# Decoder step on one core: split-array products gathered into fewer interruptions of the dense matmul stream

## Chip, core, metric

One core of one Trainium2 chip runs the whole step. The metric is the device time of one execution, in microseconds (us). The chip's TensorE is called PE below, with its weight loads PEld; DVE is VectorE, ACT ScalarE, POOL GpSimd, SP the engine that issues DMAs.

## What is computed

One decoder layer on 512 prompt tokens and 8 sample tokens with 2048 tokens of past each:

```python
(conv), (q, k, v), (qd, kd, vd), gates = in_projection(rmsnorm(h), w_in)
y_a = conv_mixer(...)                      # gated width-3 convolution
z = q.k / 8 + b_h                          # stick-breaking attention, 8 heads, strictly causal
a = exp(log_sigmoid(z) + sum of log_sigmoid(-z) over later keys);  y_b = (a @ v) @ w_br_sb
y_c = combine of three dilated softmax windows (128,1), (512,4), (2048,16), 4 heads each
h = h + (g0*y_a + g1*y_b + g2*y_c) @ w_out
h = h + relu(rmsnorm(h) @ w_up)**2 @ w_down
```

The prompt attends to itself; the sample tokens attend to a paged pool of keys and values (16 pages of 128 tokens for each of 8 sequences) and to the window caches. Outputs are the new hidden rows and all new keys, values and window caches.

## The kernel before

**The dense stream.** Every weight matrix is cut into tiles of 128 output columns (a unit). fp32 products are made of three fp32r products (high x high, high x low, low x high), so a unit of 8 k-tiles for one half of the 520 tokens is 24 matmuls of 128x128 by 260 columns: one *tick*. A unit is two ticks. `TICKS` is the list of all ticks, in this order: sq, sk, sv (12 units), dq, dk, dv (18), convolution (12), gates, branches, out, MLP. Ticks 0 to 59 are the projections up to dv, ticks 60 to 83 the convolution's, 84 on the gates. ACT makes the high part of a weight tile, POOL or DVE the low part, DVE takes every tick's result from one of three PSUM banks G0 to G2.

**The interruptions.** Everything else that PE does is slipped between the two halves of a tick, or behind a tick. `make_plan` (from line 282) gives every such stage a due time in ticks; the list `PLAN` has one cell per half tick, and every engine walks through it. On PE the stages of one cell are sorted by `tensor_order` (`ARRAY_PARTS`, line 379): first transposes, then sums (`p_sum`, `l_sum`), then scores (`p_scores`, `l_scores`), then the products with pages and caches. A cell with work for PE is called an interruption below. There are 91.

Four shapes of product occur in them:
- *full*: transposes (`p_turn`, `l_turn`, `sv_rows`, `dv_rows`) and the bf16 mask product of identity and mask, 128x128;
- *64 columns* (128*64 in the profile): `p_sum(r)` adds up attention weights times values for two heads, `l_sum(m)` the same for a dilated step;
- *64 rows* (64*128): `p_scores(n)`, q.k for two heads, and `l_scores(m)`, one dilated step of two heads;
- *32 columns* (128*32): `dk(i)` (queries of the sample against two K tiles, 8 products of 512 columns), `v_sum(n)` (weights against one V tile, 4 products), `s_k`, `s_self`, `s_v`, `s_vself` (the windows of the sample).

A plain fp32 product is two records in the profile.

**Order of the prompt attention.** The sequence `PSEQ` has 32 heads times query blocks and four steps "d" for the sample's K pages. Step m has scores at tick 20 + m (for two heads at once, every second step), ACT's `p_weights` at +1, DVE's `p_scan` at +1, ACT's `p_exp` at +2, PE's `p_turn` at +3, and `p_sum` at +4 of the odd head. PSUM banks: scores in S0 and S1, transposes in TR, sums in OU, 32-column products in Z. The copies of the transposed weights, `pT`, are a ring of 3.

**The dilated part** has 16 steps from tick 61 on: `l_scores(m)` at 61 + m, logits (DVE), exponentials (ACT), `l_turn` at +2, `l_sum` at +3.

**Pages.** K and V pages and window caches go through four SBUF tiles `kv` of 1 MB. SP loads tile i when stage i - 4 has been used (`kv_load`, waiting for the semaphore `kv_used`); a tile of four pages is four DMAs, with the page numbers read from SBUF before. `DK_TICK` gives the ticks of the 16 `dk` stages by hand; the 32 `v_sum` come every 1.15 ticks from tick 53 to 90, each in a cell of its own.

```python
s_t = max(t + 1.0, at("dk", 5) + 1.5)
add(t + 4, "p_sum", n // 2)
t = int(v0 + 1.15 * i + 1.5 * (i // PAGES))
add(l0 + m, "l_scores", m)
add(l0 + m + 3, "l_sum", m)
```

Of the kernel before, what the change touches and what calls it, by code (L numbers as in the profile page):

```python
# [16 lines left out]
P = 128  # L17
# [99 lines left out]
def at(kind, tile, half=1):  # L117
    return AT[kind, tile, half]
# [153 lines left out]
for _n_ in range(QB * SBH):  # L272
    if _n_ in (0, 6, 16, 24):
        PSEQ.append(("d", len([1 for s in PSEQ if s[0] == "d"])))
    PSEQ.append(("p", _n_))
M_OF = {step: m for m, step in enumerate(PSEQ)}


DK_TICK = (10, 13, 15, 18, 21, 23, 25, 26, 30, 32, 34, 36, 39, 42, 44, 46)

# [4 lines left out]
def make_plan():  # L285

    plan = [[] for _ in range(2 * NT)]

    def add(tick, stage, n=0):
        plan[int(2 * tick) + 1].append((stage, n))  # L290

    t_kv = {}
    add(at("sq", 3) + 0.5, "qz")
    for i, t in enumerate(DK_TICK):
        add(t, "dk", i)
        t_kv[2 * i] = t_kv[2 * i + 1] = t
    add(at("dq", 5) + 1, "qd_zero")
    add(at("dk", 5) + 0.5, "qd")
    s_t = max(t + 1.0, at("dk", 5) + 1.5)
    for g in range(NG):  # L300
        add(s_t + g, "s_k", g)
        t_kv[KV_SK + g] = s_t + g
    add(s_t + 2.5, "s_self")
    add(s_t + 3, "s_log")
    add(s_t + 4, "s_soft")

    for i in range(QB):
        add(at("sv", 3) + 1.5 + i, "sv_rows", i)
    s0 = 20
    for m, (what, n) in enumerate(PSEQ):  # L310
        t = s0 + m
        if what == "p" and n % 2 == 0:
            add(t, "p_scores", n)
        add(t + 0.5, "p_weights", m)
        add(t + 1, "p_scan", m)
        add(t + 2, "p_exp", m)
        add(t + 3, "p_turn", m)
        if what == "p" and n % 2:
            add(t + 4, "p_sum", n // 2)
    p_end = s0 + len(PSEQ) + 4  # L320

    for g in range(NG):
        for r in range(2):
            add(at("dv", 5) + 1.5 + 2 * g + r, "dv_rows", 2 * g + r)
    add(at("dv", 5) + 1, "dvs")

    v0 = s_t + 4.5
    for i in range(2 * PAGES):
        t = int(v0 + 1.15 * i + 1.5 * (i // PAGES))
        add(t, "v_sum", i)  # L330
        t_kv[KV_V + i] = t
        if i % PAGES == PAGES - 1:
            add(t + 0.5, "v_out", i // PAGES)
            add(t + 2, "v_red", i // PAGES)
    v_end = t
    add(at("dv", 5) + 7.5, "s_turn")
    add(at("dv", 5) + 8.5, "s_vd")
    for g in range(NG):
        t = v_end + 1.5 + g
        add(t, "s_v", g)  # L340
        t_kv[KV_SV + g] = t
    add(t + 0.5, "s_vself")
    add(t + 1, "s_vout")
    add(t + 2.5, "s_red")

    l0 = max(p_end + 1, at("dv", 5) + 2)
# [70 lines left out]
def decoder_step(nc, x, o):  # L417

    ctx = ExitStack()
    with ctx:  # L420
# [56 lines left out]
        pw = place("pw", [P, 2, 512], R + 11408)  # L477
        pT = [place("pT0", [P, 512], R + 12432), place("pT1", [P, 512], c0 + 736), place("pT2", [P, 512], R + 21248)]

# [4 lines left out]
        bias = place("bias", [P, GH, BW], R)  # L484
        lT = place("lT", [P, 2, 512], R + 2048)
        o_sub = place("o_sub", [P, GH // 2, S], R + 3072)
# [77 lines left out]
        bias_in = sem("bias_in")  # L564
        l_made, l_pmade = sem("l_made"), sem("l_pmade")
        l_less, l_power, l_share_made, l_done = sem("l_less"), sem("l_power"), sem("l_share_made"), sem("l_done")
# [289 lines left out]
        def _(act):  # L856
# [171 lines left out]
            def l_turn(m):  # L1028
                cols = 2 * P * l_step(m)[3]
                copy(lT[:, m % 2, 0:cols], await_bank(act, "l_turn", m)[:, 0:cols]).then_inc(read["TR"], 1)  # L1030

# [144 lines left out]
        def _(dve):  # L1176
# [311 lines left out]
            def p_turn(m):  # L1488
                what, n = PSEQ[m]
                if what == "p":  # L1490
                    cols = P * (n // SBH + 1)
                    nc.vector.tensor_copy(pT[n % 3][:, 0:cols], await_bank(dve, "p_turn", m)[:, 0:cols]).then_inc(read["TR"], 1)

            def l_scores(m):
                jp, sub, i, blocks = l_step(m)
                n, end = P * blocks, BW if sub else 256
                if m == 0:
# [5 lines left out]
                for e in range(2):  # L1503
                    src = await_bank(dve, "l_scores", m, e)
                    stt(logits[:, e, :], src[:, 0:n], SCALE, bias[:, 2 * jp + e, end - n:end],
                        ALU.mult, ALU.add).then_inc(of(read, "l_scores", m, e), 1)
                for e in range(2):
                    await_taken(dve, "l_scores", m, e)
                nc.vector.tensor_reduce(lstat[:, 0, sub, i, 2 * jp:2 * jp + 2], logits, AX.X, ALU.max,
# [90 lines left out]
            def h_low(t):  # L1600
# [3 lines left out]

            stages = dict(p_scan=p_scan, p_turn=p_turn, l_scores=l_scores, l_stat=l_stat, l_mul=l_mul, v_out=v_out, s_log=s_log,
                          s_soft=s_soft, s_vout=s_vout, branch_split=branch_split)
# [33 lines left out]
        def _(pe):  # L1640
# [109 lines left out]
            def dk(i):  # L1750
# [14 lines left out]
                ins.then_inc(kv_used, 2)  # L1765

            def p_scores(n):
# [8 lines left out]
                for e in range(2):  # L1776
# [11 lines left out]
            def p_sum(r):  # L1788
# [5 lines left out]
                for b in range(i + 1):  # L1794
                    for e in range(2):
                        c = P * t + HD * e
                        ins = mm(dst[HD * e:HD * e + HD, P * t:P * t + P], sv_tok[:, b, c:c + HD],
                                 pT[(2 * r + e) % 3][:, P * b:P * b + P], b == 0, b == i, tile_position=(0, HD * e))
                if t == SBH // 2 - 1:
# [95 lines left out]

            def l_scores(m):
                jp, sub, i, blocks = l_step(m)
                if m == 0:
                    pe.wait_ge(dve_took, at("dk", 5) + 1)
                dst = [open_bank(pe, "l_scores", m, e) for e in range(2)]  # L1900
                queries = slice(P * i, P * i + P)
                keys = queries if sub else slice(P * (i + 1 - blocks), P * i + P)
                for n in range(2 if sub else 1):
                    for e in range(2):
                        t, rows = head(GH * (sub + n) + 2 * jp + e)
                        out = dst[e][:, P * n:P * n + P] if sub else dst[e][:, 0:P * blocks]
                        ins = mm(out, dqT[rows, t, queries], dkT[rows, t, keys], True, True)
                        if n == sub:
                            ins.then_inc(of(written, "l_scores", m, e), 1)

# [10 lines left out]
            def l_sum(m):  # L1921
# [7 lines left out]
                for b in range(blocks):  # L1929
                    g, rows = (1 + b, i) if sub else (0, i + 1 - blocks + b)  # L1930
                    for e in range(2):
                        d0 = 256 * g + HD * (2 * jp + e)
                        c = P * (blocks * e + b)
                        ins = mm(bank["OU"][HD * e:HD * e + HD, P * i:P * i + P], dv_tok[:, rows, d0:d0 + HD],
                                 lT[:, m % 2, c:c + P], b == 0, b == blocks - 1, tile_position=(0, HD * e))
                if m % QB == QB - 1:
# [22 lines left out]

            stages = dict(sv_rows=sv_rows, dv_rows=dv_rows, dk=dk, p_scores=p_scores, p_turn=p_turn, p_sum=p_sum,  # L1960
                          v_sum=v_sum, v_red=v_red, s_k=s_k, s_self=s_self, s_turn=s_turn, s_vd=s_vd, s_v=s_v,
# [175 lines left out]
```

## Time and profile before

| | |
|---|---|
| median of 3 runs | 1022.78 us (1021.09 to 1024.04) |
| profiled execution, first to last instruction (span) | 1019.7 us |
| time of that one execution as the runs count it | not listed apart; median less span is 3.1 us |
| PE busy | 998.8 us, 98% of the span |
| DVE, ACT, POOL busy | 586.0, 440.0, 312.0 us |
| mean granted clock of PE | 0.997 of full |
| DMA | 209.49 MB, 205 GB/s on average |

A busy PE record is longer than the step from one record to the next, since matmuls overlap; what a matmul costs the stream is the difference between its start and the next one's start. The timeline view prints those starts.

### The profile page before, as it was taken

How to read it: one execution, taken by the hardware profiler on the slowest of the kernel's cores; microseconds unless marked ns; L12 is line 12 of the kernel's file. 1: busy time of each engine (PE TensorE's matmuls, PEld its weight loads, DVE VectorE, ACT ScalarE, POOL GpSimd, SP SyncE). 2: the span in 40 equal slices, each digit the busy share in tenths (PEclk: the TensorE clock that was granted, in tenths of full speed). 3: DMA queues.
4: the chain of work that ended last, by engine and by line, in shares of the span. 5: the costliest groups of instructions: out<-in, count | busy, mean ns of one | idle time of the engine just before them, and what ended most of it. 6: DMA issues, size and time to landing. Idle time of an engine off the chain costs nothing.

```text
span 1019.7 us, 21807 instructions
## 1 busy us (share of the span) xinstructions
PE 998.8 (98%) x8426; PEld 912.7 (90%) x8426; DVE 586.0 (57%) x1042; ACT 440.0 (43%) x858; POOL 312.0 (31%) x180
## 2 busy tenths in 40 slices
PE   7999999999999999999999999999999999999996
PEld 6988787787877776899999999999999999999996
DVE  6215467879355457234445485577937956873334
ACT  6115556677244432234233323465436436434532
POOL 2333233222211221111112111144634355364720
PEclk9999999999999999999999999999999999999998
DMA  8589876785976467723322325456577487469102
GB/s 298 187 269 319 326 257 224 264 272 179 308 276 199 160 225 250 279 68 125 141 93 84 103 84 179 184 196 248 217 279 269 174 291 270 152 253 369 63 1 84
DMA packets 65672, 209.49 MB, mean 205 GB/s; under 512 B 7833, under 2 KB 10138, under 8 KB 63266
## 3 DMA queue, kind: packets, MB, share of 16 engines
q1 hardware_dynamic: 65282, 207.75, 57.9%
q8 instruction: 68, 1.11, 0.4%
q10 hardware_dynamic: 288, 0.35, 0.2%
q14 instruction: 34, 0.28, 0.1%
HBM read 200.59 MB, written 51.48 MB: 247 GB/s over the span
## 4 chain that ended last, share of the span: by engine, by line
PE 92%; DVE 3%; issue 1%; DMA 1%; SPq 1%; ACT 1%; DVEq 0%; ACTq 0%
PE G L1642 61%; PE S L1642 14%; PE Z L1642 13%; PE OU L1642 2%; PE TR L1645 2%; DMA kv<-in_kpool_dram 1%; DMA xraw<-in_xt_dram 1%; DVE mtmp L1188 1%; PE TR L1642 0%; DVE macc L1185 0%; DVE convy L1188 0%; SPq L720 0%; DVE pw L1483 0%; ACT mixh L865 0%; DVE wlo L1185 0%
## 5 line engine op out<-in xcount | busy, mean ns | idle before, releaser
L1642 PE MATMUL G<-xh,whi 128*128 128x260 f32 x1288 | 373.9, 290 | 8.1 <-DVE xl L1188 7.3
L1642 PE MATMUL G<-xl,whi 128*128 128x260 f32 x1288 | 364.9, 283 | 0.0
L1642 PE MATMUL G<-xh,wlo 128*128 128x260 f32 x1288 | 364.4, 283 | 0.0
L831 POOL TENSOR_TENSOR wlo<-wraw,whi 128x1024 fp32r<-128x1024 f32 x60 | 147.4, 2457 | 490.8 <-ACT whi L865 490.8
L1642 PEld LDWEIGHTS G<-xh,whi 128*128 128x128 f32 x1288 | 243.3, 189 | 52.2 <-issue 50.5
L1642 PEld LDWEIGHTS G<-xl,whi 128*128 128x128 f32 x1288 | 243.5, 189 | 0.0
L1642 PEld LDWEIGHTS G<-xh,wlo 128*128 128x128 f32 x1288 | 243.5, 189 | 0.0
L865 ACT ACTIVATE whi<-wraw 128x1024 fp32r<-128x1024 f32 (+1 forms) x84 | 88.0, 1048 | 226.1 <-PE G L1642 213.2
L827 POOL TENSOR_TENSOR wlo<-mraw,whi 128x512 fp32r<-128x512 f32 x60 | 81.6, 1382 | 95.1 <-ACT whi L865 95.1
L841 POOL TENSOR_TENSOR mlow<-mraw,bhigh 128x512 fp32r<-128x512 f32 x36 | 57.6, 1620 | 66.1 <-DVE bsum L1185 59.1
L1185 DVE TENSOR_TENSOR tg<-G,rstd 128x260 f32<-128x260 f32 x48 | 20.5, 428 | 85.8 <-PE G L1642 85.8
L1185 DVE TENSOR_TENSOR slow<-bsum,bhigh 128x512 fp32r<-128x512 f32 x48 | 60.1, 1252 | 3.0 <-ACT bhigh L865 3.0
L1642 PE MATMUL S<-xl,whi 128*128 128x260 f32 x176 | 49.7, 282 | 0.0
L1642 PE MATMUL S<-xh,whi 128*128 128x260 f32 x176 | 49.7, 282 | 0.0
L1642 PE MATMUL S<-xh,wlo 128*128 128x260 f32 x176 | 49.7, 282 | 0.0
L865 ACT ACTIVATE whi<-mraw 128x512 fp32r<-128x512 f32 (+1 forms) x62 | 36.3, 637 | 26.5 <-PE G L1642 9.5
L1483 DVE TENSOR_TENSOR_SCAN pw<-psp 128x512 f32<-128x512 f32 (+3 forms) x33 | 46.4, 1405 | 1.1
L1642 PE MATMUL G<-binh,whi 128*128 128x260 f32 x160 | 45.7, 285 | 1.3 <-issue 1.3
L923 ACT ACTIVATE tg<-tg,cvec 128x260 f32<-128x260 f32 x48 | 24.2, 505 | 49.5 <-DVE tg L1185 49.5
L1642 PE MATMUL G<-binh,wlo 128*128 128x260 f32 x160 | 45.3, 283 | 0.0
L1642 PE MATMUL G<-binl,whi 128*128 128x260 f32 x160 | 45.3, 283 | 0.0
L865 ACT ACTIVATE bhigh<-bsum 128x512 fp32r<-128x512 f32 x48 | 30.2, 630 | 32.4 <-DVE bsum L1185 32.0
(329 smaller groups left out, 2233.4 us busy)
## 6 DMA issues: line engine op xcount, KB each, us to landing
wraw<-in_w_in_dram SPq DMA_DIRECT2D x65, 512.0 KB, 5.8
kv<-in_kpool_dram SPq DMA_DIRECT2D x128, 256.0 KB, 3.8
kv<-in_vpool_dram SPq DMA_DIRECT2D x128, 256.0 KB, 3.5
mraw<-in_w_up_dram SPq DMA_DIRECT2D x32, 512.0 KB, 5.0
out_win_k_kept_dram<-in_cache_win_k_dram SPq DMA_DIRECT2D x8, 2047.0 KB, 11.4
out_win_v_kept_dram<-in_cache_win_v_dram SPq DMA_DIRECT2D x8, 2047.0 KB, 10.6
mraw<-in_w_down_dram SPq DMA_DIRECT2D x30, 512.0 KB, 3.4
wraw<-in_w_ab_dram SPq DMA_DIRECT2D x8, 512.0 KB, 3.3
```

The lines of the kernel that those rows point to most:

```text
L827: nc.gpsimd.tensor_tensor(low(u)[:, part], raw(u)[0][:, part], high(u)[:, part].bitcast(F32), ALU.subtract).then_inc(w_lo, 1)
L831: nc.gpsimd.tensor_tensor(low(u), raw(u)[0], high(u).bitcast(F32), ALU.subtract).then_inc(w_lo, 1)
L841: nc.gpsimd.tensor_tensor(block_low(g, j), block_raw(g, j), block_high(g, j).bitcast(F32), ALU.subtract).then_inc(b_lo_pool, 1)
L865: return nc.scalar.activation(out, in_, ACT.Copy, **kw)
L923: nc.scalar.activation(part, part, ACT.Tanh, scale=0.5, bias=bgate[:, g, t:t + 1]).then_inc(tanh_made, 1)
L1185: return nc.vector.tensor_tensor(out, a, b, op)
L1188: return nc.vector.scalar_tensor_tensor(out, a, scalar, b, op0, op1)
L1483: link(nc.vector.tensor_tensor_scan(w_[:, ::-1], l[:, ::-1], l[:, ::-1], carry, ALU.add, ALU.bypass))
L1642: return nc.tensor.matmul(out, lhsT, rhs, start=start, stop=stop, **kw)
L1645: return nc.tensor.transpose(out, in_, ident[0:rows, 0:rows])
```

## The change

Ticks of the plan: PSEQ's "d" steps move (8 in place of 6), `dk` 4 to 15 are put on ticks of `p_scores`; `p_sum` waits for the next cell that has split-array work (`TILED_TICKS`); the three `s_k` and `s_self` share tick 50, the three `s_v` and `s_vself` tick 92; V pages go in pairs, on three ticks of the prompt and on each pair of dilated steps, then every third tick; dilated steps go in pairs, with both steps' scores in one bank (columns 0 to 255 and 256 to 511) and both sums two ticks later. The mask product comes before the scores, which then add to it. `pT` is a ring of 5, `lT` of 3.

```diff
-    if _n_ in (0, 6, 16, 24):
+    if _n_ in (0, 8, 16, 24):
...
-DK_TICK = (10, 13, 15, 18, 21, 23, 25, 26, 30, 32, 34, 36, 39, 42, 44, 46)
+S0_TICK = 20
+SCORE_TICK = [S0_TICK + M_OF["p", 2 * r] for r in range(QB * SBH // 2)]
+TILED_TICKS = SCORE_TICK + [SCORE_TICK[-1] + 3, SCORE_TICK[-1] + 5]
+SUM_TICK = [min(t for t in TILED_TICKS if t >= SCORE_TICK[r] + 5) for r in range(QB * SBH // 2)]
+DK_TICK = [10, 13, 15, 18] + SCORE_TICK[0:12]
+PT_RING = 5
...
-    s_t = max(t + 1.0, at("dk", 5) + 1.5)
+    s_t = SCORE_TICK[13]
     for g in range(NG):
-        add(s_t + g, "s_k", g)
-        t_kv[KV_SK + g] = s_t + g
-    add(s_t + 2.5, "s_self")
+        add(s_t, "s_k", g)
+        t_kv[KV_SK + g] = s_t
+    add(s_t, "s_self")
...
         if what == "p" and n % 2 == 0:
+            add(t, "p_mask", n)
             add(t, "p_scores", n)
...
-            add(t + 4, "p_sum", n // 2)
+            add(SUM_TICK[n // 2], "p_sum", n // 2)
...
-    v0 = s_t + 4.5
+    l0 = max(p_end + 1, at("dv", 5) + 2)
+    v_ticks = [SCORE_TICK[-1]] + TILED_TICKS[-2:] + [l0 + 2 * q for q in range(LSTEPS // 2)]
+    while len(v_ticks) < PAGES:
+        v_ticks.append(v_ticks[-1] + 3)
     for i in range(2 * PAGES):
-        t = int(v0 + 1.15 * i + 1.5 * (i // PAGES))
+        t = v_ticks[i // 2]
         add(t, "v_sum", i)
...
     for g in range(NG):
-        t = v_end + 1.5 + g
+        t = v_end + 2
         add(t, "s_v", g)
...
-    for m in range(LSTEPS):
-        add(l0 + m, "l_scores", m)
-        add(l0 + m + 1, "l_weights", m)
-        add(l0 + m + 3, "l_sum", m)
-        if m % QB == QB - 1:
-            add(l0 + m + 3, "l_out", m // QB)
-        add(l0 + m + 2, "l_turn", m)
+    for q in range(LSTEPS // 2):
+        t = l0 + 2 * q
+        add(t, "l_scores", q)
+        for m in (2 * q, 2 * q + 1):
+            late = 0.5 * (m % 2)
+            add(t + late, "l_logits", m)
+            add(t + 1 + late, "l_weights", m)
+            add(t + 2 + 2 * late, "l_turn", m)
+            add(t + 4, "l_sum", m)
+            if m % QB == QB - 1:
+                add(t + 4, "l_out", m // QB)
...
+            def p_mask(n):
+                keys = P * (n // SBH + 1)
+                for e in range(2):
+                    dst = open_bank(pe, "p_scores", n + e)
+                    mm(dst[:, keys - P:keys], identb[:], maskb[:], True, True)
...
-                dst = [open_bank(pe, "p_scores", n + e) for e in range(2)]
                 for e in range(2):
                     t, rows = head((n + e) % SBH)
-                    mm(dst[e][:, 0:keys], sqT[rows, t, P * i:P * i + P], skT[rows, t, 0:keys], True, False)
-                for e in range(2):
-                    mm(dst[e][:, keys - P:keys], identb[:], maskb[:], False,
-                       True).then_inc(of(written, "p_scores", n + e), 1)
+                    dst = bank[SPOT["p_scores", n + e][0]]
+                    mm(dst[:, 0:keys], sqT[rows, t, P * i:P * i + P], skT[rows, t, 0:keys], False, True,
+                       skip_group_check=True).then_inc(of(written, "p_scores", n + e), 1)
...
-                        if n == sub:
-                            ins.then_inc(of(written, "l_scores", m, e), 1)
+                            if m % 2 and n == sub:
+                                ins.then_inc(of(written, "l_scores", q, e), 1)
```

DVE's stage that makes the logits, before called `l_scores` too, is now `l_logits`; it reads columns 256 * (m % 2) on, and frees the bank after the second step.

## Rows read from the trace of the kernel before

**Rows 1.** The page: busy time by engine, and the granted clock in 40 slices.

```profile
PE 998.8 (98%) x8426; PEld 912.7 (90%) x8426; DVE 586.0 (57%) x1042; ACT 440.0 (43%) x858; POOL 312.0 (31%) x180
...
PEclk9999999999999999999999999999999999999998
```

**Rows 2.** Timeline of PE (start us, duration us, instruction): the interruption at 298 us.

```profile
298.22 0.28 PE L1642 MATMUL G<-xh,wlo 128*128 128x260 f32 x1
298.34 0.60 PE L1645 MATMUL TR<-ident,lg 128*128 128x128 f32 x4
298.87 0.66 PE L1642 MATMUL OU<-lT,dv_tok 128*64 128x128 f32 x8
299.46 0.71 PE L1642 MATMUL S<-dkT,dqT 64*128 64x128 f32 x8
300.10 1.07 PE L1642 MATMUL Z<-kv,wT 128*32 128x512 f32 x8
301.10 0.39 PE L1642 MATMUL G<-xh,whi 128*128 128x260 f32 x1
301.32 0.29 PE L1642 MATMUL G<-xl,whi 128*128 128x260 f32 x1
```

**Rows 3.** Timeline of PE: the interruption at 152 us, with mask product and K pages.

```profile
152.65 0.38 PE L1645 MATMUL TR<-ident,pw 128*128 128x128 f32 x2
152.96 0.70 PE L1642 MATMUL S<-skT,sqT 64*128 64x256 f32 x4
153.59 0.28 PE L1642 MATMUL S<-maskb,identb 128*128 128x128 bf16 x2
153.81 1.93 PE L1642 MATMUL Z<-kv,qz 128*32 128x512 f32 x16
155.66 0.39 PE L1642 MATMUL G<-xh,whi 128*128 128x260 f32 x1
```

**Rows 4.** Timeline of PE: the ends of the interruptions at 231 and 236 us.

```profile
232.01 1.13 PE L1642 MATMUL S<-skT,sqT 64*128 64x512 f32 x4
233.07 0.28 PE L1642 MATMUL S<-maskb,identb 128*128 128x128 bf16 x2
233.17 0.37 PE L1642 MATMUL G<-xh,whi 128*128 128x260 f32 x1
...
237.03 1.09 PE L1642 MATMUL OU<-pT,sv_tok 128*64 128x128 f32 x16
238.06 1.07 PE L1642 MATMUL Z<-kv,wT 128*32 128x512 f32 x8
```

**Rows 5.** Timeline of PE: an interruption of transposes alone, at 162 us.

```profile
162.53 0.38 PE L1645 MATMUL TR<-ident,pw 128*128 128x128 f32 x2
162.67 0.37 PE L1642 MATMUL G<-xh,whi 128*128 128x260 f32 x1
162.87 0.28 PE L1642 MATMUL G<-xl,whi 128*128 128x260 f32 x1
```

**Rows 6.** Waits of PE: who waited for whom, us in total, times, longest.

```profile
PE Z L1642 <- DMA kv<-in_kpool_dram: 0.7, 1, 0.7
PE S L1642 <- DVE lg L1188: 0.5, 1, 0.5
...
PE TR L1645 <- DVE pT L1492: 0.2, 1, 0.2
```

**Rows 7.** SP's timeline for one pair of K tiles, and landings of V pages (last: median us).

```profile
46.31 5.96 SPq L720 DMA_DIRECT2D kv<-in_kpool_dram  x8
...
kv<-in_vpool_dram SPq DMA_DIRECT2D x128, 256.0 KB, 3.5
```

**Rows 8.** Instructions on tile lg: duration ns min/median/max, first and last start us.

```profile
L1188 DVE SCALAR_TENSOR_TENSOR lg<-S,bias x32: 282/415/426, 277.1 to 363.1; 128x256 f32<-128x256 f32 x28, 128x128 f32<-128x128 f32 x4
```

**Rows 9.** Timeline of PE near the start of the kernel.

```profile
8.06 0.42 PE L1642 MATMUL G<-xl,whi 128*128 128x260 f32 x1
8.28 0.42 PE L1642 MATMUL G<-xh,wlo 128*128 128x260 f32 x1
```

More of the change, by code:

```diff
@@ L298, in make_plan @@
     add(at("dk", 5) + 0.5, "qd")
-    s_t = max(t + 1.0, at("dk", 5) + 1.5)
+    s_t = SCORE_TICK[13]
     for g in range(NG):
-        add(s_t + g, "s_k", g)
-        t_kv[KV_SK + g] = s_t + g
-    add(s_t + 2.5, "s_self")
-    add(s_t + 3, "s_log")
-    add(s_t + 4, "s_soft")
+        add(s_t, "s_k", g)
+        t_kv[KV_SK + g] = s_t
+    add(s_t, "s_self")
+    add(s_t + 0.5, "s_log")
+    add(s_t + 1.5, "s_soft")
     for i in range(QB):
         add(at("sv", 3) + 1.5 + i, "sv_rows", i)
-    s0 = 20
+    s0 = S0_TICK
     for m, (what, n) in enumerate(PSEQ):
@@ L338, in make_plan @@
     for g in range(NG):
-        t = v_end + 1.5 + g
+        t = v_end + 2
         add(t, "s_v", g)
         t_kv[KV_SV + g] = t
[L342 to L346, printed above, removed]
+    add(t, "s_vself")
+    add(t + 0.5, "s_vout")
+    add(t + 2, "s_red")
     add(l0 - 3, "bias_load")
-    for m in range(LSTEPS):
-        add(l0 + m, "l_scores", m)
-        add(l0 + m + 1, "l_weights", m)
-        add(l0 + m + 3, "l_sum", m)
-        if m % QB == QB - 1:
-            add(l0 + m + 3, "l_out", m // QB)
-        add(l0 + m + 2, "l_turn", m)
+    for q in range(LSTEPS // 2):
[9 more added lines that the diff above has]
+                add(t + 4, "l_out", m // QB)
     t = l0 + LSTEPS
@@ L477, in decoder_step @@
         pw = place("pw", [P, 2, 512], R + 11408)
-        pT = [place("pT0", [P, 512], R + 12432), place("pT1", [P, 512], c0 + 736), place("pT2", [P, 512], R + 21248)]
+        pT = [place("pT0", [P, 512], R + 12432), place("pT1", [P, 512], c0 + 736)]
+        pT += [place(f"pT{2 + i}", [P, 512], R + 20720 + 512 * i) for i in range(PT_RING - 2)]
         dqT = place("dqT", [P, 6, TOK], R + 12944)
@@ L484, in decoder_step @@
         bias = place("bias", [P, GH, BW], R)
-        lT = place("lT", [P, 2, 512], R + 2048)
+        lT = [place("lT0", [P, 512], R + 2048), place("lT1", [P, 512], R + 2560), place("lT2", [P, 512], R + 11408)]
         o_sub = place("o_sub", [P, GH // 2, S], R + 3072)
@@ L564, in decoder_step @@
         bias_in = sem("bias_in")
-        l_made, l_pmade = sem("l_made"), sem("l_pmade")
+        l_first_made, l_made, l_pmade = sem("l_first_made"), sem("l_made"), sem("l_pmade")
         l_less, l_power, l_share_made, l_done = sem("l_less"), sem("l_power"), sem("l_share_made"), sem("l_done")
@@ L1029, in l_turn @@
                 cols = 2 * P * l_step(m)[3]
-                copy(lT[:, m % 2, 0:cols], await_bank(act, "l_turn", m)[:, 0:cols]).then_inc(read["TR"], 1)
+                copy(lT[m % 3][:, 0:cols], await_bank(act, "l_turn", m)[:, 0:cols]).then_inc(read["TR"], 1)
             def l_out(n):
@@ L1491, in p_turn, with l_logits @@
                     cols = P * (n // SBH + 1)
-                    nc.vector.tensor_copy(pT[n % 3][:, 0:cols], await_bank(dve, "p_turn", m)[:, 0:cols]).then_inc(read["TR"], 1)
-            def l_scores(m):
+                    nc.vector.tensor_copy(pT[n % PT_RING][:, 0:cols], await_bank(dve, "p_turn", m)[:, 0:cols]).then_inc(read["TR"], 1)
+            def l_logits(m):
                 jp, sub, i, blocks = l_step(m)
-                n, end = P * blocks, BW if sub else 256
+                n, end, second = P * blocks, BW if sub else 256, m % 2
                 if m == 0:
@@ L1503, in l_scores @@
                 for e in range(2):
-                    src = await_bank(dve, "l_scores", m, e)
-                    stt(logits[:, e, :], src[:, 0:n], SCALE, bias[:, 2 * jp + e, end - n:end],
-                        ALU.mult, ALU.add).then_inc(of(read, "l_scores", m, e), 1)
-                for e in range(2):
-                    await_taken(dve, "l_scores", m, e)
+                    src = await_bank(dve, "l_scores", m // 2, e)
+                    stt(logits[:, e, :], src[:, 256 * second:256 * second + n], SCALE, bias[:, 2 * jp + e, end - n:end],
+                        ALU.mult, ALU.add).then_inc(of(read, "l_scores", m // 2, e) if second else l_first_made, 1)
+                if second:
+                    for e in range(2):
+                        await_taken(dve, "l_scores", m // 2, e)
+                else:
+                    dve.wait_ge(l_first_made, m + 2)
                 nc.vector.tensor_reduce(lstat[:, 0, sub, i, 2 * jp:2 * jp + 2], logits, AX.X, ALU.max,
@@ L1603, in h_low @@
                     ALU.subtract).then_inc(hn_lo, 1)
-            stages = dict(p_scan=p_scan, p_turn=p_turn, l_scores=l_scores, l_stat=l_stat, l_mul=l_mul, v_out=v_out, s_log=s_log,
+            stages = dict(p_scan=p_scan, p_turn=p_turn, l_logits=l_logits, l_stat=l_stat, l_mul=l_mul, v_out=v_out, s_log=s_log,
                           s_soft=s_soft, s_vout=s_vout, branch_split=branch_split)
@@ L1765, in dk @@
                 ins.then_inc(kv_used, 2)
+            def p_mask(n):
+                keys = P * (n // SBH + 1)
+                for e in range(2):
+                    dst = open_bank(pe, "p_scores", n + e)
+                    mm(dst[:, keys - P:keys], identb[:], maskb[:], True, True)
             def p_scores(n):
@@ L1771, in p_scores @@
                     pe.wait_ge(dve_took, at("sk", 3) + 1)
-                dst = [open_bank(pe, "p_scores", n + e) for e in range(2)]
                 for e in range(2):
                     t, rows = head((n + e) % SBH)
-                    mm(dst[e][:, 0:keys], sqT[rows, t, P * i:P * i + P], skT[rows, t, 0:keys], True, False)
-                for e in range(2):
-                    mm(dst[e][:, keys - P:keys], identb[:], maskb[:], False,
-                       True).then_inc(of(written, "p_scores", n + e), 1)
+                    dst = bank[SPOT["p_scores", n + e][0]]
+                    mm(dst[:, 0:keys], sqT[rows, t, P * i:P * i + P], skT[rows, t, 0:keys], False, True,
+                       skip_group_check=True).then_inc(of(written, "p_scores", n + e), 1)
             def p_turn(m):
@@ L1797, in p_sum @@
                         ins = mm(dst[HD * e:HD * e + HD, P * t:P * t + P], sv_tok[:, b, c:c + HD],
-                                 pT[(2 * r + e) % 3][:, P * b:P * b + P], b == 0, b == i, tile_position=(0, HD * e))
+                                 pT[(2 * r + e) % PT_RING][:, P * b:P * b + P], b == 0, b == i, tile_position=(0, HD * e))
                 if t == SBH // 2 - 1:
@@ L1894, in s_red, with l_scores @@
                 ins.then_inc(written["TR"], 1)
-            def l_scores(m):
-                jp, sub, i, blocks = l_step(m)
-                if m == 0:
+            def l_scores(q):
+                if q == 0:
                     pe.wait_ge(dve_took, at("dk", 5) + 1)
[L1900 to L1907, printed above, removed]
-                        if n == sub:
-                            ins.then_inc(of(written, "l_scores", m, e), 1)
+                dst = [open_bank(pe, "l_scores", q, e) for e in range(2)]
+                for m in (2 * q, 2 * q + 1):
+                    jp, sub, i, blocks = l_step(m)
+                    c = 256 * (m % 2)
+                    queries = slice(P * i, P * i + P)
+                    keys = queries if sub else slice(P * (i + 1 - blocks), P * i + P)
+                    for n in range(2 if sub else 1):
+                        for e in range(2):
+                            t, rows = head(GH * (sub + n) + 2 * jp + e)
+                            out = dst[e][:, c + P * n:c + P * n + P] if sub else dst[e][:, c:c + P * blocks]
+                            ins = mm(out, dqT[rows, t, queries], dkT[rows, t, keys], True, True)
+                            if m % 2 and n == sub:
+                                ins.then_inc(of(written, "l_scores", q, e), 1)
             def l_turn(m):
@@ L1934, in l_sum @@
                         ins = mm(bank["OU"][HD * e:HD * e + HD, P * i:P * i + P], dv_tok[:, rows, d0:d0 + HD],
-                                 lT[:, m % 2, c:c + P], b == 0, b == blocks - 1, tile_position=(0, HD * e))
+                                 lT[m % 3][:, c:c + P], b == 0, b == blocks - 1, tile_position=(0, HD * e))
                 if m % QB == QB - 1:
@@ L1958, in l_mul @@
                     ins.then_inc(of(written, "l_mul", jp, sub), 1)
-            stages = dict(sv_rows=sv_rows, dv_rows=dv_rows, dk=dk, p_scores=p_scores, p_turn=p_turn, p_sum=p_sum,
+            stages = dict(sv_rows=sv_rows, dv_rows=dv_rows, dk=dk, p_mask=p_mask, p_scores=p_scores, p_turn=p_turn, p_sum=p_sum,
                           v_sum=v_sum, v_red=v_red, s_k=s_k, s_self=s_self, s_turn=s_turn, s_vd=s_vd, s_v=s_v,
```

## Prediction

> **What bounds the kernel now.** I read the page first: PE is busy for 98% of the span, no other engine for more than 57%, and its granted clock stands at full in nearly every slice [rows 1]. So time is won only by taking time out of PE's own stream, and the stream has to be read by the starts of its matmuls. In the timeline of one interruption [rows 2] the last dense matmul starts at 298.22 and the next instruction 0.12 us later: that is the dense step, and a tick of 24 is 2.9 us. Then come four shapes one after the other, and the first dense matmul at 301.10 holds up the second by 0.22 instead of 0.12. The list of PE's waits is short: between 30 and 450 us only three entries concern this change, 0.7, 0.5 and 0.2 us [rows 6]. So an interruption costs what PE itself needs for it, and what other engines do lies beside the stream, as long as nothing there becomes late.
>
> **The price of one interruption, taken apart.** Within one shape the time has a part that grows with the columns and a part that doesn't.
> - 32 columns: 8 records take 1.00 us (300.10 to 301.10 [rows 2]), 16 take 1.85 (153.81 to 155.66 [rows 3]). So 0.85 us per 8, and 0.15 us once.
> - 64 columns: 8 records 0.59 [rows 2], 16 records 1.03 [rows 4]: 0.44 per 8, and 0.15 once.
> - 64 rows: four records of 256 columns 0.63 [rows 3], of 512 columns 1.06 [rows 4]: 0.43 per 256, and 0.20 once.
> - Way in and out: two transposes before dense work take 0.14, and the dense step behind them 0.20, 0.08 too much [rows 5]; that is 0.11 per transpose and nothing once. The same two before split work take 0.31 [rows 3], 0.17 more, and the dense step behind split work is 0.22 [rows 2], 0.02 more than behind transposes. So an interruption with split work costs 0.19 us beyond its parts.
> - The mask product after the scores, with dense work behind it: 0.10 [rows 4]; with K pages behind it: 0.22 [rows 3]. Between two split shapes it costs 0.12 us more, since the array goes to the full shape and back.
>
> **The change part by part.** I count cells by evaluating the tick lists of the diff; the work in columns is the same before and after.
> 1. *Fewer interruptions with split work.* Before: 69 of 91 (the other 22 are transposes alone). After: 39 of 79: 4 early dk, 16 scores, 2 sums behind the prompt's, 8 dilated pairs, l_sum at ticks 77 and 79, V at 78, 81, 84, 87 and 90, l_mul at 83 (84 shares V's cell), s_v at 92. That is 4+16+2+8+2+5+1+1 = 39. 30 fewer, at 0.19: 5.7 us. The transposes left alone on their ticks (40 such cells) cost 0.11 each as before.
> 2. *Runs of the 32-column shape:* before 16 dk, 32 V, 3 s_k, s_self, 3 s_v, s_vself = 56; after 16 dk, 16 V, 1, 1 = 34. 22 at 0.15: 3.3 us.
> 3. *Runs of the 64-column shape:* before 16 p_sum, 16 l_sum, 2 l_mul = 34; after 12 cells with p_sum, 8 with l_sum, 2 = 22. 12 at 0.15: 1.8 us.
> 4. *Runs of the 64-row shape:* before 16 + 16, after 16 + 8. 8 at 0.20: 1.6 us.
> 5. *Mask ahead of the scores.* Before, in 9 of the 16 cells the mask stood between two split shapes: 9 times 0.12, 1.1 us. In the other 7 nothing is saved on that side, and the way out costs 0.02 more: 0.1 us back. Whether a mask behind transposes and ahead of scores has a joint of its own no row shows. The bounds: it costs its 0.10 and the 0.12 of the rows above (no gain, 0 us over 16 cells), or it takes over the 0.17 that the transposes pay now (up to 16 x 0.17 = 2.7 us). I take 1.0 us, since transposes are the nearest full-shape neighbour.
> 6. *Two stages of one shape joined.* The rows show 16 records in a run only from a single stage. Joined stages wait on semaphores in between. The bounds: nothing, as inside dk's 16 records, which themselves come from two tiles, or the whole fixed part again. I take nothing, by dk's row [rows 3], which is the nearest; the other end is a rival.
> 7. *Waits that go.* dk 7, now at tick 26, waited 0.7 us for its K pages; at tick 27 it has 2.9 us more. The scores of dilated step 3 waited 0.5 us for DVE to empty S0, because the convolution's operations stood ahead; a pair leaves two ticks. The transposes at tick 53 waited 0.2 for DVE's copy, with s_log ahead of it; s_log moves away by more than a tick [rows 6]. 1.4 us. v_red meets the transposes of a dilated step in the bank TR before and after: no change.
>
> Sum: 5.7 + 3.3 + 1.8 + 1.6 + 1.0 + 1.4 = **14.8 us**. The profiled execution has a span of 1019.7; against the median of 1022.8 that leaves 3.1 us around it, which stay. 1022.8 - 14.8 = **1008.0 us**, a span of 1004.9.
>
> **What costs nothing, and its cover.**
> - *The pages.* A V tile is loaded when the stage four tiles back is through, so a pair's loads start when the pair two before is through. Two tiles take SP 6.0 us to issue, and the last DMA lands 3.5 us later [rows 7]; with a reading of page numbers ahead, which no row shows and for which I allow 2 us, 11 to 12 us. Between those two pairs lie 4 ticks (11.6 us), one interruption of 4.4 us and three cells of transposes (0.4 each): 17 us. About 5 us of cover; if it is gone, PE waits at its pair. The weight load behind a pair in SP's queue starts up to 7 us later than before, but its unit is needed more than 5 ticks on. The last s_v tile is released at tick 90 and needed at the end of tick 92, behind v_red and two other s_v: 5.8 + 0.9 + 2 x 0.85 + 0.85 = 9 us for one load.
> - *The dilated chain.* DVE has two logits of 0.42 each per step [rows 8], then a maximum, then ACT two exponentials. A pair doubles that, but its first transpose comes two ticks and the V products later (1.7 + 5.8 + 0.4 = 8 us), its second a tick after. The score banks must be free two ticks on.
> - *p_sum up to two ticks late* is what the ring of 5 is for; its last sum stays on tick 59, so nothing behind it moves.
> - *New wait in DVE's queue:* s_log at tick 51 now waits for the end of an interruption of 5.7 us; behind it stands the take of tick 51, which is due 2.9 us after that end anyway.
> - *Mask products* open the score banks up to 1 us earlier; ACT emptied them in the tick before.
>
> **The rivals.**
> - *A joined stage pays again* (item 6). Then the 22 + 12 + 8 = 42 joints give back 34 x 0.15 + 8 x 0.20 = 6.7 us: 1014.7. For it: every run now in the trace is one stage. Against: within dk two products of different tiles follow each other without a mark. The Trainium skill, TensorEngine Tiling (Array Packing), Key Properties, says that the array is drained on a change of the tiling mode and not of the tile; by that rule this rival falls, and no run yet shows it.
> - *Pages late.* If pair loads took 1 us longer than their cover at each of 12 pairs, 12 us would come back: 1020. For it: DMA moves two tiles at once. Against: the cover of 5 us, and K pages run in pairs now with one wait in 16 [rows 6]. A smaller form, a few waits of 1 us, gives 1010 to 1013.
> - *Slower: the clock falls.* 13 interruptions last longer than 4 us, up to 5.7, where the one at 152 us takes 3.0 (152.65 to 155.66 [rows 3]); work in them uses only part of the array. Near the start dense matmuls come every 0.22 us (8.06 to 8.28 [rows 9]), 260 columns at the lower level of 1.2 GHz, against 0.12 at 2.4. If one tick behind each of the 13 ran so, that is 13 x 24 x 0.10 = 31 us: 1039. It decides from 14.8 / 13 = 1.1 us each, 11 matmuls at the lower level. Against: the clock stays full in slices where an interruption comes every 5 to 6 us [rows 1]. The Trainium skill, TensorE: Matmul & The Clock Gate, Part 1, describes a gate that follows the engine's activity; the row agrees so far, as it falls for none of the interruptions shown.
> - *The fixed parts are no cost of the shape change* but of something that stays, such as the first product's fetch. Items 1 to 4 would shrink as in the first rival; it has the same price and shares its chance.
>
> **How the numbers follow.** Forecast 0.81, joined stages pay 0.08, pages or another engine late 0.07, clock 0.04. The forecast's own spread: item 5 up to 1.7 us more or 1.0 less, the median of three runs 1.5 either way: 1005 to 1011. With the smaller form of late pages and a part of the first rival the range is 1005.0 to 1013.0. A change of 0.3% (3 us) is about what a measurement of this kernel can tell from none. All cases but the clock and the worst of late pages are faster by more than that: faster 0.94, same 0.02, slower 0.04.
>
> **What would show it.** In the changed profile V products stand in runs of 16 records over 1.85 us, not 2.00; l_sum in runs of 16 over 1.03; scores of a pair over 1.06; a pure transpose cell stays at 0.11 per transpose. The mask's row stands ahead of the scores, and K pages follow the scores directly. PE's waits for kv and lg are gone and no new ones over 1 us are there. Dense steps stay at 0.12. Joints of 0.15 inside the runs, waits on DMA kv, or dense steps of 0.22 would make it wrong.

## The result, and the profile of the changed kernel

The changed kernel takes 1009.08 us in the median of 4 runs (1008.92 to 1010.09), the kernel before 1022.83 in 4. The ratio is 0.9871, with a 95% interval of 0.9859 to 0.9883. That is 13.8 us less, where 14.8 were forecast, and inside the range. The span of the profiled execution falls by 12.9 us, from 1019.7 to 1006.8, and its own time is 1010.09.

The page's first lines and the granted clock, answering to [rows 1]:

```profile
span 1006.8 us, 21775 instructions
...
PE 986.1 (98%) x8426; PEld 914.7 (91%) x8426; DVE 587.9 (58%) x1042; ACT 439.8 (44%) x858; POOL 312.6 (31%) x180
...
PEclk9999999999999999999999999999999999999999
```

The number of PE records is the same, 8426: nothing was taken out but the room between them. The clock stayed at its higher level.

One interruption of the dilated part, timeline of PE, which answers to [rows 2]:

```profile
301.96 0.28 PE L1658 MATMUL G<-xh,wlo 128*128 128x260 f32 x1
302.08 0.60 PE L1661 MATMUL TR<-ident,lg 128*128 128x128 f32 x4
302.61 1.09 PE L1658 MATMUL OU<-lT,dv_tok 128*64 128x128 f32 x16
303.63 1.16 PE L1658 MATMUL S<-dkT,dqT 64*128 64x128 f32 x16
304.73 1.92 PE L1658 MATMUL Z<-kv,wT 128*32 128x512 f32 x16
306.58 0.39 PE L1658 MATMUL G<-xh,whi 128*128 128x260 f32 x1
306.81 0.28 PE L1658 MATMUL G<-xl,whi 128*128 128x260 f32 x1
```

Each shape now has two stages' records in one run. The V products of two tiles take 1.85 us (304.73 to 306.58), where one tile took 1.00 before [rows 2]; the sums of two steps 1.02 where one step's took 0.59; the scores of two steps 1.10 where one step's took 0.64. A run of 16 is what one stage's columns twice and one fixed part make, within 0.02 us: the joints inside the runs cost nothing.

One interruption of the prompt's part, with the mask ahead, which answers to [rows 3]:

```profile
150.05 0.38 PE L1661 MATMUL TR<-ident,pw 128*128 128x128 f32 x2
150.26 0.27 PE L1658 MATMUL S<-maskb,identb 128*128 128x128 bf16 x2
150.47 0.66 PE L1658 MATMUL OU<-pT,sv_tok 128*64 128x128 f32 x8
151.06 0.70 PE L1658 MATMUL S<-skT,sqT 64*128 64x256 f32 x4
151.69 1.92 PE L1658 MATMUL Z<-kv,qz 128*32 128x512 f32 x16
153.54 0.39 PE L1658 MATMUL G<-xh,whi 128*128 128x260 f32 x1
```

Two transposes and the mask take 0.42 us together (150.05 to 150.47). Before, the transposes took 0.31 and the mask behind the scores 0.22 [rows 3], so 0.11 is gone.

PE's waits in the changed kernel, which answer to [rows 6]:

```profile
...
PE TR L1661 <- DVE pT L1505: 1.2, 2, 0.8
PE OU L1658 <- DVE yacc L1198: 1.0, 1, 1.0
PE TR L1661 <- ACT o_sbT L878: 0.6, 1, 0.6
...
PE G L1658 <- DVE convu L1198: 0.3, 1, 0.3
```

The waits on the K pages and on DVE's reading of S are gone. The one on pT, 0.2 in one place before [rows 6], has grown to 1.2 in two places. This is the interruption at tick 57:

```profile
249.76 0.28 PE L1658 MATMUL G<-xh,wlo 128*128 128x260 f32 x1
250.80 0.63 PE L1661 MATMUL TR<-ident,pw 128*128 128x128 f32 x4 [0.76 <-DVE pT L1505]
251.36 1.97 PE L1658 MATMUL OU<-pT,sv_tok 128*64 128x128 f32 x32
253.25 1.92 PE L1658 MATMUL Z<-kv,wT 128*32 128x512 f32 x16
```

From the last dense start to the transposes 1.04 us pass instead of 0.12: 0.92 us lost, of which the row shows 0.76 as idle, since a record's modelled end lies behind the next step's start. At tick 54 it is 0.57.

**Where the time went, added up.** I took each interruption from the last dense start ahead of it to the second dense start behind it, less two dense steps. The 91 of before sum to 159.4 us, the 79 of now to 146.5: 12.9 us, the whole difference of the spans. Priced by the fixed parts of the prediction and without any wait, they give 157.4 and 144.0, that is 13.4 us. What stands above its price is mostly waits. Before, it is 0.8 us at tick 26 (K pages), 0.4 at tick 53 (pT), 0.5 at tick 64 (S) and 0.5 at tick 72 (the bank TR); now it is 0.6 at tick 54, 0.9 at tick 57 (both pT) and 0.7 at tick 71 (TR). That is 2.2 us on either side, so the waits together gave nothing. The shapes gave the 12.9; the 0.5 us that they fell short of their price is spread over many split interruptions, at 0.03 to 0.11 each.

### The profile page after: what moved, and what is told of

The parts are those of the page before. It is cut to its first block, busy times and chain, and to the rows that moved or that the text cites. A ratio compares the mean times of both kernels' runs of the same rounds, so it can differ in the third digit from the quotient of the medians.

```text
span 1006.8 us, 21775 instructions
## 1 busy us (share of the span) xinstructions
PE 986.1 (98%) x8426; PEld 914.7 (91%) x8426; DVE 587.9 (58%) x1042; ACT 439.8 (44%) x858; POOL 312.6 (31%) x180
## 4 chain that ended last, share of the span: by engine, by line
PE 93%; DVE 4%; issue 1%; ACT 1%; DMA 0%; DVEq 0%; ACTq 0%
PE G L1658 61%; PE S L1658 14%; PE Z L1658 13%; PE TR L1661 2%; PE OU L1658 2%; DVE pw L1496 1%; DVE mtmp L1201 1%; DMA xraw<-in_xt_dram 0%; DVE macc L1198 0%; DVE psp L1201 0%; PE TR L1658 0%; DVE share L1547 0%; DVE dvT L1198 0%; ACT mixh L878 0%; DVE pT L1505 0%
```

## The experiments

All of them are compared with the changed kernel (1009.08 us; sum of interruptions 146.5) unless the text says otherwise. The experiments ran later than the changed kernel, and the kernel before, run beside them, came to 1022.54, 1022.36 and 1021.87 us where it had 1022.83. So a difference of about 1 us between medians decides nothing here; what decides is the sum of the interruptions, and the waits, in each trace. Four runs have a single execution.

**1. The mask alone** (`mask_first`), in the kernel before:

```diff
+            add(t, "p_mask", n)
             add(t, "p_scores", n)
...
-                    mm(dst[e][:, keys - P:keys], identb[:], maskb[:], False,
-                       True).then_inc(of(written, "p_scores", n + e), 1)
+            def p_mask(n):
+                keys = P * (n // SBH + 1)
+                for e in range(2):
+                    dst = open_bank(pe, "p_scores", n + e)
+                    mm(dst[:, keys - P:keys], identb[:], maskb[:], True, True)
```

> The kernel before with one part alone: the mask product stands ahead of the scores. My theory (a shape change costs a fixed amount, and the mask between two split shapes costs one change more): the 9 interruptions in which K or V pages follow get 0.1 us shorter, the 7 others stay within 0.03; about 0.8 us in all, so a ratio near 0.999. Rival (the mask ahead takes over the way in from the transposes): each of the 16 gets up to 0.17 shorter, 2.7 us in all.

Measured: 1021.64 us against 1022.54, ratio 0.9991 (0.9981 to 1.0000). The interval just reaches 1, so the times don't decide it. Interruption by interruption in the trace, the 8 with pages behind and nothing moved but the mask are 0.09 to 0.11 shorter, the 6 with dense work behind 0.03 longer. The one at 152 us, timeline of PE, against [rows 3]:

```profile
152.50 0.38 PE L1646 MATMUL TR<-ident,pw 128*128 128x128 f32 x2
152.71 0.27 PE L1643 MATMUL S<-maskb,identb 128*128 128x128 bf16 x2
152.92 0.70 PE L1643 MATMUL S<-skT,sqT 64*128 64x256 f32 x4
153.55 1.92 PE L1643 MATMUL Z<-kv,qz 128*32 128x512 f32 x16
155.40 0.39 PE L1643 MATMUL G<-xh,whi 128*128 128x260 f32 x1
```

2.90 us from 152.50 to 155.40, against 3.01 before. Of the last two of the 16, at ticks 52 and 54, the first is 0.03 longer like its kind, and the other carries a wait of 1.2 us for DVE's copy of pT; the kernel before had 0.4 of it one tick earlier. That wait hides what the shapes gain there. It comes from a small operation of DVE that starts just behind POOL's. First the kernel before, then this one, timelines of DVE and POOL:

```profile
239.48 0.18 DVE L1185 TENSOR_TENSOR sself<-slog,cvec 128x24 f32<-128x24 f32 x1
239.48 2.45 POOL L831 TENSOR_TENSOR wlo<-wraw,whi 128x1024 fp32r<-128x1024 f32 x1 [7.83 <-ACT whi L865]
```

```profile
239.30 2.43 DVE L1186 TENSOR_TENSOR sself<-slog,cvec 128x24 f32<-128x24 f32 x1
239.29 2.41 POOL L832 TENSOR_TENSOR wlo<-wraw,whi 128x1024 fp32r<-128x1024 f32 x1 [7.83 <-ACT whi L866]
```

The same operation takes 0.18 us in one and 2.43 in the other, and all that DVE has to do behind it comes later (experiment 5 returns to this). So the size of these waits can hang on hundredths of a us.

By shapes alone the mask is worth 9 x 0.10 - 7 x 0.03 = 0.7 us, near the theory's 0.8 and far from the rival's 2.7. With the new wait and 0.2 us more at tick 26 the profiled execution's interruptions sum to 160.2, 0.8 more than before, though the median of the runs is 0.9 lower; so the timed runs can't be said to show the 0.7, only the single interruptions do. The wait is a first hint at DVE and POOL.

**2. V pages split around the other shapes** (`v_around`):

```diff
-    return ARRAY_PARTS.get(stage[0], 0)
+    return 0.5 if stage[0] == "v_sum" and stage[1] % 2 == 0 else ARRAY_PARTS.get(stage[0], 0)
```

> The changed kernel, but in each interruption the first V page of a pair comes before the sums and scores and the second after them. Same stages, same waits, same columns. Where the pair shares its interruption with sums or scores (14 of 16 pairs), there is one run of the 32-column shape more. My theory (only a change of shape costs): 14 x 0.15 = 2.1 us longer. Rival (a stage costs its fixed part wherever it stands): no change, and V stages of 1.00 us each also where two are joined.

Measured: 1010.59 us, 1.5 more; against the kernel before 0.9879 (0.9863 to 0.9896). My count was wrong: 11 pairs share an interruption with sums or scores, not 14. Of these, nine are longer by 0.14 us each and the two at ticks 54 and 57 by 0.12 and 0.11, in all 1.5 us; the rest are unchanged within 0.02. The same interruption as above:

```profile
303.74 0.60 PE L1661 MATMUL TR<-ident,lg 128*128 128x128 f32 x4
304.26 1.06 PE L1658 MATMUL Z<-kv,wT 128*32 128x512 f32 x8
305.26 1.09 PE L1658 MATMUL OU<-lT,dv_tok 128*64 128x128 f32 x16
306.29 1.16 PE L1658 MATMUL S<-dkT,dqT 64*128 64x128 f32 x16
307.38 1.06 PE L1658 MATMUL Z<-kv,wT 128*32 128x512 f32 x8
308.37 0.39 PE L1658 MATMUL G<-xh,whi 128*128 128x260 f32 x1
```

1.00 and 0.99 us for the two V stages apart, 1.85 when joined. The same stages, waits and columns cost more only because another shape stands between them. This settles the rival that a joined stage pays again, and the one that the fixed part belongs to the stage.

**3. V pages unpaired** (`v_single`):

```diff
-        t = v_ticks[i // 2]
+        t = v_ticks[i // 2] - 1 + i % 2
```

> The changed kernel with V pages unpaired: the first of a pair one tick earlier. 16 runs of the 32-column shape more, 0.15 each = 2.4 us, and 14 cells of transposes alone (or empty) become split interruptions, 0.19 each = 2.7 us. If the waits of 0.6 and 0.9 us at ticks 54 and 57 come from bare ticks in which DVE has more to do than PE, they shrink to nothing here, 1.5 us back: in all 3.6 us longer than the changed kernel. If those waits have another cause, 5.1 us longer.

Measured: 1012.70 us, 3.6 more; against before 0.9899 (0.9883 to 0.9916). The waits on pT are gone. One of 0.6 us is new: the first V product of the second half comes one tick after the last of the first half, and waits for DVE to empty the bank Z.

```profile
PE Z L1658 <- DVE scol L1571: 0.6, 1, 0.6
PE TR L1661 <- ACT o_sbT L878: 0.6, 1, 0.6
```

The interruptions sum to 150.6, 4.1 more: about 5.1 for shapes and 0.6 for the new wait, less 1.5 of the waits that went. Had these stayed, it would be 5.7.

**4. Less work for DVE** (`dve_less`):

```diff
-                link(nc.vector.tensor_tensor_scan(w_[:, ::-1], l[:, ::-1], l[:, ::-1], carry, ALU.add, ALU.bypass))
+                scan = nc.vector.tensor_tensor_scan(w_[:, ::-1], l[:, ::-1], l[:, ::-1], carry, ALU.add, ALU.bypass)
+                if what == "p" and n >= 26:
+                    scan.then_inc(p_wmade, 1)
+                    return
+                link(scan)
```

> The changed kernel without DVE's last step of the scan stage (cumulated minus z) for the prompt's heads 26 to 31; this leaves out 0.69 us of DVE work in six ticks. Theory (DVE is the pace in the bare ticks 51 to 57, and PE's transposes wait for its copies and scans): the waits before the transposes of ticks 54 and 57, together 1.5 us, fall below 0.3. Rival (ACT is the pace, which has as much to do per tick): they stay above 1 us.

Measured, one execution: 1007.44 us. The wait at tick 54 is gone and the one at tick 57 is 0.2 us instead of 0.92 (0.32 from dense start to transposes). All other interruptions are the same within 0.02 us, and their sum is 1.3 lower. ACT's work was not touched, so ACT as the pace falls.

**5. Less work for POOL** (`pool_less`):

```diff
+                part = slice(0, 1) if 26 <= u <= 31 else slice(0, KC)
-                nc.gpsimd.tensor_tensor(low(u), raw(u)[0], high(u).bitcast(F32), ALU.subtract).then_inc(w_lo, 1)
+                nc.gpsimd.tensor_tensor(low(u)[:, part], raw(u)[0][:, part], high(u)[:, part].bitcast(F32),
+                                        ALU.subtract).then_inc(w_lo, 1)
```

> The changed kernel, but POOL makes only one eighth of the low parts of weight units 26 to 31 (the rest of those low parts is left as it was, so part of the projection is left out). DVE's scans of 512 keys take 1.2 us alone and 3.3 us where POOL's weight operation of 2.4 us runs beside them. Theory (POOL's operation holds up DVE, and DVE is the pace at ticks 51 to 57): no operation of DVE between 224 and 256 us takes over 1.4 us, and PE's waits before the transposes of ticks 54 and 57 (1.5 us together) go to below 0.2. Rival (DVE's own work is too much for a bare tick even alone, 3.7 against 3.3 us): the waits stay above half.

Measured, one execution: 1007.72 us; both waits on pT are gone entirely, the sum of interruptions is 1.55 lower. DVE did all its work. First DVE and POOL in the changed kernel, timeline:

```profile
225.76 3.31 DVE L1496 TENSOR_TENSOR_SCAN pw<-psp 128x512 f32<-128x512 f32 x1
...
244.81 2.81 DVE L1201 SCALAR_TENSOR_TENSOR psp<-pz,psp 128x512 f32<-128x512 f32 x1
247.65 1.22 DVE L1496 TENSOR_TENSOR_SCAN pw<-psp 128x512 f32<-128x512 f32 x1
```

```profile
225.20 2.79 POOL L844 TENSOR_TENSOR wlo<-wraw,whi 128x1024 fp32r<-128x1024 f32 x1 [9.35 <-ACT whi L878]
...
244.66 2.40 POOL L844 TENSOR_TENSOR wlo<-wraw,whi 128x1024 fp32r<-128x1024 f32 x1 [8.22 <-ACT whi L878]
```

and then DVE in this experiment:

```profile
226.25 1.37 DVE L1498 TENSOR_TENSOR_SCAN pw<-psp 128x512 f32<-128x512 f32 x1
...
244.71 0.86 DVE L1203 SCALAR_TENSOR_TENSOR psp<-pz,psp 128x512 f32<-128x512 f32 x1
245.61 1.23 DVE L1498 TENSOR_TENSOR_SCAN pw<-psp 128x512 f32<-128x512 f32 x1
```

The scan that starts beside POOL's operation takes 3.31 us there and 1.37 here, the other operation 2.81 and 0.86; POOL's own take at most 0.85 here. So these DVE operations, started under POOL's, end about as late as if they had begun when POOL was through. The Trainium skill, SBUF — State Buffer, SBUF: two separate sides, says that a DVE operation with two SBUF inputs and a GpSimd operation that reads SBUF hold a shared port pair exclusively: the one that starts first has it for the whole instruction, and the other waits. Both DVE operations have two SBUF inputs, and the rows agree. So do two others of the changed kernel: the copy of pT, which reads PSUM, takes its usual 0.68 us in the middle of POOL's operation, and the operation with two SBUF inputs behind it takes 1.55.

```profile
234.06 2.39 POOL L844 TENSOR_TENSOR wlo<-wraw,whi 128x1024 fp32r<-128x1024 f32 x1 [6.08 <-ACT whi L878]
234.85 0.68 DVE L1505 COPY pT<-TR 128x512 f32<-128x512 f32 x1
235.44 1.55 DVE L1201 SCALAR_TENSOR_TENSOR psp<-pz,psp 128x512 f32<-128x512 f32 x1
```

**6. and 7. Other orders of the shapes** (`scores_first`, `scores_last`): the scores' place among the shapes 1 and 3 instead of 2, by the numbers in `ARRAY_PARTS`.

```diff
-ARRAY_PARTS = dict(p_sum=1, l_sum=1, p_scores=2, l_scores=2, dk=3, v_sum=3, s_k=3, s_self=3, s_v=3, s_vself=3)
+ARRAY_PARTS = dict(p_sum=2, l_sum=2, p_scores=1, l_scores=1, dk=3, v_sum=3, s_k=3, s_self=3, s_v=3, s_vself=3)
```

> The changed kernel with the scores ahead of the sums in each interruption. Same shapes, same number of runs. If each run has its own fixed part (0.15, 0.20, 0.15 us) whatever stands beside it, PE's interruptions keep their sum within 0.3 us. Rival (the 0.20 of the 64-row shape belongs to the joint with its neighbours): the sum moves by 0.05 for each of the 18 interruptions that have both, 0.9 us either way.

> The changed kernel with K and V pages ahead of the scores, which come last before the dense matmuls. By fixed parts of their own the sum stays within 0.3 us of the changed kernel's. Rival (it depends on what follows): 23 interruptions move by 0.05 each, about 1.1 us. Scores 1.7 us later leave ACT and DVE less time, so waits may grow at ticks 52 to 57.

Measured, one execution each: 1009.00 and 1008.59 us, sums of interruptions 146.50 and 146.52 against 146.54. No interruption moves by more than 0.02 us. The fixed part, 0.20 for 64 rows and 0.15 for 64 or 32 columns, belongs to the run and not to its neighbours; as long as each shape stays in one run, the order is free.

**8. The sums not gathered** (`sum_own`):

```diff
-SUM_TICK = [min(t for t in TILED_TICKS if t >= SCORE_TICK[r] + 5) for r in range(QB * SBH // 2)]
+SUM_TICK = [SCORE_TICK[r] + 5 for r in range(QB * SBH // 2)]
```

> The changed kernel with the prompt's sums at their earliest tick, as before, and not gathered. 8 sums (ticks 26, 28, 35, 37, 44, 46, 53, 55) make interruptions of transposes into split ones, 0.19 each = 1.5 us, and there are 4 runs of the 64-column shape more, 0.15 each = 0.6 us: 2.1 us. The sums at 53 and 55 fill two ticks that are bare in the changed kernel, so DVE's backlog shrinks and of the waits at 54 and 57 (1.5 us) at least half goes: in all 0.6 to 1.4 us longer than the changed kernel. If the backlog explanation is wrong, the waits stay and it is 2.1 us longer.

Measured: 1009.59 us, 0.5 more; against before 0.9888 (0.9871 to 0.9904). Sum of interruptions 147.1, 0.6 more. No wait on pT is left: 2.1 us of shapes less 1.5 us of waits is 0.6. The kernel before had a sum and a V page on each of ticks 53 and 55, and the change took both away; the sums alone, put back, are enough to make the waits go.

**9. A version that beats both** (`spread`):

```diff
-    v_ticks = [SCORE_TICK[-1]] + TILED_TICKS[-2:] + [l0 + 2 * q for q in range(LSTEPS // 2)]
-    while len(v_ticks) < PAGES:
-        v_ticks.append(v_ticks[-1] + 3)
+    v_ticks = [53, 55, 57, 59] + [l0 + 2 * q for q in range(LSTEPS // 2)] + [77, 79, 83, 90]
...
-            add(t + 2, "v_red", i // PAGES)
+            add(t + 2.5, "v_red", i // PAGES)
```

> A version meant to beat both: V pairs at ticks 53, 55, 57, 59, on the dilated pairs, then 77, 79, 83 and 90, so that ticks 53 and 55 aren't bare and three late pairs share the interruption of sums; v_red half a tick later, so that it doesn't meet the dilated transposes in the bank TR. One split interruption less (0.2), waits of 0.6, 0.9 and 0.7 us go: 2.4 us shorter than the changed kernel, 1006.7. Rival (DVE's backlog only moves to a later tick): the waits come back at ticks 57 to 59, and 0.9 us is won.

Measured: 1006.32 us in the median of 5 (1005.85 to 1007.59), ratio to before 0.9845 (0.9826 to 0.9865). Its waits:

```profile
...
PE G L1656 <- issue: 1.3, 3, 0.7
PE OU L1656 <- DVE yacc L1196: 1.0, 1, 1.0
PE G L1656 <- DVE sqT L1196: 0.5, 1, 0.5
PE G L1656 <- DVE wlo L1196: 0.4, 1, 0.4
```

Neither pT nor the bank TR is in the list, and the interruptions sum to 144.2, 2.3 less than the changed kernel's, where 2.4 was expected. The transposes of tick 57 start one dense step after the last dense matmul:

```profile
251.64 0.28 PE L1656 MATMUL G<-xh,wlo 128*128 128x260 f32 x1
251.76 0.60 PE L1659 MATMUL TR<-ident,pw 128*128 128x128 f32 x4
```

So the backlog did not move on: V products put where DVE needs the time cost PE nothing that it wouldn't spend anyway. The gain over the changed kernel is clear by the sum. By the timed runs, each taken against the kernel before beside it, it is 0.9845 against 0.9871, and the two intervals still overlap a little.

## Why the prediction was right, and where it was off

- *Items 1 to 4, fewer interruptions and runs* (12.4 us): right. The counts 69 to 39, 56 to 34, 34 to 22 and 32 to 24 hold, and interruptions priced that way meet every one of the changed kernel within 0.11 us but three, which carry waits. The small excesses run one way and add up to 0.5 us, so that items 1 to 6 gave 12.9 us where 13.4 was forecast. Experiments 2, 6 and 7 show that the fixed part is one per run and depends on nothing else tried.
- *Item 5, the mask* (1.0 us): 0.7 by the single interruptions of experiment 1. The mask has no joint with the transposes ahead of it, and takes none of their way in over; the 1.0 stood nearer to the truth than either bound, 0 and 2.7.
- *Item 6, joined stages* (nothing): right, 1.85 us for two.
- *Item 7, waits that go* (1.4 us): this is the step that failed. The waits on the K pages and on S went, 1.3 us as measured from dense starts. The third, on DVE's copy at tick 53, I took to come from s_log standing ahead. With s_log moved away, it came back at ticks 54 and 57 with 0.6 and 0.9 us, 1.1 us more than before; with 0.2 more in the bank TR (below) that ate all that the other two gave. My section on covers has a line for pages, for the dilated chain, for sums and for s_log, and none for the prompt's own chain on DVE in ticks 51 to 58. There DVE has, per tick, a take, a copy, and three operations of 512 columns, and every second tick POOL's weight operation beside it. The trace of the kernel before shows the collision of the two, ahead of the very wait that I put down to s_log alone:

```profile
228.85 2.80 POOL L831 TENSOR_TENSOR wlo<-wraw,whi 128x1024 fp32r<-128x1024 f32 x1 [8.54 <-ACT whi L865]
229.42 3.31 DVE L1483 TENSOR_TENSOR_SCAN pw<-psp 128x512 f32<-128x512 f32 x1
```

In the kernel before each of these ticks held an interruption of 1.2 us or more (up to 3.1) with split-array work; the change left transposes alone, 0.4 us, on five of them (51, 53, 55, 56 and 58). Experiments 3, 5, 8 and 9 each remove the wait on pT in another way, and experiment 4 all but 0.2 us of it. The meeting of v_red and the transposes in the bank TR cost 0.5 before and 0.7 now, where I wrote no change; half a tick apart it costs nothing (experiment 9).
- *Pages:* cover as forecast. No wait on kv. From the last landing to first use, V pairs have 4.8 us or more (5 was forecast); the tightest tile in the whole kernel is K's at tick 27, with 2.7, which had 0.1 before.
- *The clock:* did not fall. The mean is 0.998, and it is 1.00 in the 8 us (214 to 222) that hold the interruption of 5.8 us at tick 50. The Trainium skill, TensorE: Matmul & The Clock Gate, Part 1, describes a gate that follows the engine's activity; interruptions full of split-array work, at these lengths, did not trip it here.
- *The shapes as the cause:* the Trainium skill's TensorEngine Tiling (Array Packing), Key Properties, says that a change of the mode drains the array and a change of tile doesn't. The runs agree: products of two V tiles in a row have no joint between them, and in experiment 2 one more change of shape costs 0.14 us. That the time goes into a drain no run here shows.

In sum: the shapes gave 12.9 us where 13.4 was forecast, and the waits nothing where 1.4 was forecast. A wait of 0.3 us for a late take by DVE (convu, in the list above) stands outside the interruptions, and other steps there make up for it. So the spans differ by 12.9, which is 1.9 less than the 14.8 forecast; the medians differ by 13.8. The 0.9 between them lies within the runs' spread, and it is luck that the forecast looks closer by the median than its terms were.

The 3.1 us around the span are no fixed part either. They are the median of some executions less the span of another. In more than 60 executions with both numbers the difference is 1.8 to 2.1 us; only the profiled one of the changed kernel has 3.3. It cancels in the forecast's difference and did no harm.

## What to carry to other kernels

When one engine's stream is the bound, price its odd jobs by start-to-start times and split each price into a part per column and a part per change of array shape; then gather jobs of one shape, and the saving can be counted before anything runs. But an interruption of the bounding engine is also time in which the others catch up: before emptying a stretch of it, add up what the other engines must do per unit of that stretch, with the operations that get in each other's way at their long durations. If one of them has more than the bare unit allows, put the gathered work there and not elsewhere.

## What was not expected of the hardware

- The order of the shapes doesn't matter while each stays in one run: three orders agree within 0.04 us in the sum of 79 interruptions.
- Two bf16 mask products behind transposes and ahead of a split shape add 0.11 us, no more than their two times 128 columns (0.06 each, at the dense step's 0.12 for 260); full-shape work of another type joins a run of transposes without a joint.
- DVE's operations of 512 columns took 1.2 or 3.3 us (scan) and 0.7 or 2.8 us by whether they began under POOL's operation of 2.4 to 2.8 us; with POOL's cut to 0.5 us they took 1.4 and 0.9 at the most in those ticks. An operation of DVE that started 0.01 us behind POOL's took 2.43 us, and 0.18 where the two started together (experiment 1).
